# First transfers in another order, and the squares of x added in pairs on GpSimd

## The chip, the cores and the metric

The kernel runs on one core of a Trainium2 chip. What counts is its time on the device in microseconds (us), the median of several runs. The kernel before took 2918.81 us (three runs, 2916.25 to 2926.74).

## The reference

Two transformer layers follow each other over 1024 tokens of width 1024, in float32. The first, `hybrid_layer`, begins with a modulation that is worked out from a vector c, and with an RMS norm of x; everything else in it depends on the normed and modulated h:

```
mod = (jax.nn.silu(c) @ w_ada + b_ada)[:, None, :]
shift, scale, gate = jnp.split(mod, 3, axis=-1)
h = rms_norm(x, norm_g) * (1.0 + scale) + shift
(a_q, a_kv, ...) = jnp.split(h @ w_in, IN_OFFSETS, axis=-1)
```

`rms_norm` divides each token by the root of the mean of its squares over the 1024 channels. After that come four branches (compressed, selected and windowed attention; windowed attention with a sink; stick-breaking attention; retention), gated merges and an output product. The second layer has a convolution, forgetting attention, pooling, an output product, an MLP of width 4096 and a gated embedding. The change touches only what lies ahead of the first product with `w_in`.

## The kernel before, in words

Data lie transposed: channels on the 128 partitions, tokens along the row, so that x is eight chunks of 128 channels by 1024 tokens (`mm`). A dense product takes a block of weights (128 output channels) through all eight chunks. To reach float32 accuracy, weights and operand are each split in a rounded part and a rest (`whi`, `wlo`; `xhi`, `xlo`), and every product is three matmuls (`three`, L653). ScalarE makes `whi` from the landed block `raw` (L1112), GpSimd subtracts it from `raw` to make `wlo` (L1472).

Each engine has its own program; a list of events, `TIMELINE`, written out by `list_timeline`, gives all of them the same order after the start. The first event is `norm1`, then come the blocks `Dv0` and `Dv1`, interleaved by chunks. Semaphores connect the engines. Loads are issued by SyncE (SP) on one queue, in the order of its code; where SP waits for a semaphore, all later loads wait with it.

The start, ahead of `TIMELINE`, is what the change rewrites:

- SP loads the small vectors `vec`, the whole table `tab` (identity, ones, masks, distances, 2470 columns), the modulation weights `ada1` for the scale in two halves, x as one transfer, `ada0` for the shift in two halves, and the first weight block. The second weight block goes to the same place `raw` and waits until GpSimd has subtracted the first (`w_lo`); behind it stand `rtab` and the weights `ada2` of the gate.
- VectorE makes three bfloat16 masks (L1988 to L1990), then the products of the modulation: for each of eight chunks, `ada_sum` gains `ada` times an entry of silu(c) (L2004 first, then L2006). Between the fourth and the fifth product of `ada0` it waits for the root and takes its reciprocal (L1999).
- ScalarE squares the eight chunks of x into a ring of three buffers (`chunk_square`, L1132), then takes the root (`std`, L1139) and splits the first weight block.
- TensorE sums `ada_sum` over partitions (`modulation`, L986: eight matmuls with a column of ones), then the squares of each chunk as they come (`chunk_sum`, `square_sums`, L731: eight matmuls a chunk, each shown as two records), spreads the reciprocal root over the partitions (`broadcast`, L757) and sums the other modulation.
- In `norm1`, VectorE scales each chunk by the factor and the spread row (L2080), ScalarE adds the shift (L1402, L1397), and both with GpSimd make `xhi` and `xlo` (L2086, L1115, L1479).

Of the kernel before, what the change touches and what calls it, by code (L numbers as in the profile page):

```python
# [6 lines left out]
ALU = mybir.AluOpType  # L7
# [311 lines left out]

def table_layout():  # L320
    at, out = 0, {}
    for name, n in [("dist", S), ("ident", P), ("strict", P), ("tri", P), ("negones", P), ("ones", P),
                    ("up", P), ("low", P), ("cdist", NB * NCMP), ("cmask", NB * NCMP), ("gc", 2),
                    ("eps6", 1), ("eps5", 1), ("invw", 2), ("invc", 32)]:
        out[name] = (at, n)
        at += n
    return out, at


TABLES, NTABLE = table_layout()  # L330
VECS = {}
_at = 0
for _n, _w in [("c", 8), ("b_ada", 24), ("norm_g", 8), ("final_g", 8), ("g_mix_pre", 8), ("g_mix_post", 8),
# [10 lines left out]
def build(nc, xT, pT, wstream, wada, vecs, tables, rtables, cw1, cw2, wpw, wpool, out):  # L344
    with ExitStack() as ctx:
# [3 lines left out]
        def at(name, kib, shape, dt=F32):  # L349
            return nc.alloc_sbuf_tensor_at(name, shape, dt, offset=base + int(kib * 1024))  # L350
# [4 lines left out]
        def sem(name):  # L355
            return ctx.enter_context(nc.semaphore(name))
# [6 lines left out]
        ada1 = at("ada1", 32, [P, 8, D])  # L363
        mm = at("mm", 64, [P, NC, S])
        raw = at("raw", 96, [P, 10 * P])
        whi = [at("whi%d" % i, 101 + 5 * i, [P, 10, P], F32R) for i in range(2)]
        wlo = [at("wlo%d" % i, 111 + 5 * i, [P, 10, P], F32R) for i in range(2)]
        yhi = at("yhi", 121, [P, 2, S], F32R)
# [101 lines left out]
        res_dram = nc.dram_tensor("res_dram", [P, NC, S], F32, kind="Internal").ap()  # L470


        small_in, x_in, raw_in, rtab_in = (sem(n) for n in ("small_in", "x_in", "raw_in", "rtab_in"))
        ada_in = [[sem("ada_in%d%d" % (i, half)) for half in range(2)] for i in range(3)]
# [95 lines left out]
        @block.sync  # L570
        def _(sp):
            sp.dma_start(vec[:], vecs).then_inc(small_in, 16)
            sp.dma_start(tab[:], tables).then_inc(small_in, 16)
            for half in range(2):
                sp.dma_start(ada1[:, 4 * half:4 * half + 4, :], wada[1][:, 4 * half:4 * half + 4, :]
                             ).then_inc(ada_in[1][half], 16)
            sp.dma_start(mm[:], xT).then_inc(x_in, 16)
            for half in range(2):
                sp.dma_start(ada0[:, 4 * half:4 * half + 4, :], wada[0][:, 4 * half:4 * half + 4, :]
                             ).then_inc(ada_in[0][half], 16)  # L580

            def load_weights(b):
                if b >= 1:
                    sp.wait_ge(w_lo, b)
                n = BLOCK_LEN[b]
                src = wstream[BLOCK_OFF[b]:BLOCK_OFF[b] + P * n].rearrange("(p n) -> p n", p=P)
                sp.dma_start(raw[:, 0:n], src).then_inc(raw_in, 16)

            load_weights(0)
            load_weights(1)  # L590
            sp.dma_start(rtab[:], rtables).then_inc(rtab_in, 16)
            for half in range(2):
                sp.dma_start(ada2[half][:], wada[2][:, :, half * HALF:(half + 1) * HALF]).then_inc(ada_in[2][half], 16)
            for ev in TIMELINE:
                if ev[0] == "dense" and ev[2] == 2 and 1 < ev[1] + 1 < nblocks:
                    load_weights(ev[1] + 1)
                elif ev == ("cmp", 0):

                    sp.wait_ge(k_y, H)
                    sp.dma_start(cw1s[:], cw1).then_inc(cmp_in, 16)  # L600
                    sp.dma_start(cw2s[:], cw2).then_inc(cmp_in, 16)
                elif ev == ("dense", INDEX["o0"], 3):
                    for n in range(NC):
                        wait_split(sp, 1, n)
                        sp.dma_start(mm[:, n, :], xT[:, n, :]).then_inc(xres_in[n], 16)
                elif ev == ("dense", INDEX["Ecb1"], 4):
                    for n in range(NC):
                        sp.wait_ge(chunk_ready, n + 1)
                        sp.dma_start(res_dram[:, n, :], mm[:, n, :]).then_inc(res_out, 16)
                elif ev == ("conf", 0):  # L610

                    sp.wait_ge(s_norm, 128)
                    sp.dma_start(wpws[:], wpw).then_inc(pw_in, 16)
                    sp.dma_start(wpls[:], wpool).then_inc(pw_in, 16)
                elif ev[0] == "dense" and ev[2] == 3 and BLOCKS[ev[1]][1] == "x1":
                    sp.wait_ge(res_out, 16 * NC)
# [18 lines left out]
        def _(pe):  # L635
# [346 lines left out]
            def modulation(t):  # L982
# [122 lines left out]
        @block.scalar  # L1105
        def _(act):
            def split_weights(b):
                act.wait_ge(raw_in, 16 * (b + 1))
# [3 lines left out]
                nc.scalar.activation(flat(whi[b % 2])[:, 0:n], raw[:, 0:n], ACT.Copy).then_inc(w_hi, 1)  # L1112
# [12 lines left out]

            def chunk_square(j, n, src):

                if n < 3 and j:
                    act.wait_ge(nsum, (0, 4, 6)[j])
                if n >= 3:  # L1130
                    act.wait_ge(pq_used, 7 * j + n - 2)
# [334 lines left out]
        def _(pool):  # L1466
            tt = nc.gpsimd.tensor_tensor

            def split_weights(b):
                n = BLOCK_LEN[b]  # L1470
                pool.wait_ge(w_hi, b + 1)
                tt(flat(wlo[b % 2])[:, 0:n], raw[:, 0:n], flat(whi[b % 2])[:, 0:n].bitcast(F32),  # L1472
                   ALU.subtract).then_inc(w_lo, 1)

            def split_wide(v, pos, k, src):
# [27 lines left out]
            def window_sums():  # L1503
# [5 lines left out]
                for step in range(2):  # L1509
# [122 lines left out]
        def _(dve):  # L1632
# [359 lines left out]
            v.tensor_scalar(nsink[:], v_("sink"), -1.0, None, ALU.mult).then_inc(masks_done, 1)  # L1992

            def ada_products(t, tiles):

# [16 lines left out]

            dve.wait_ge(csil_done, 1)
            for t, a in ((1, ada1), (0, ada0)):
                ada_products(t, [[(slice(0, D), a[:, kc, :], kc // 4)] for kc in range(8)])
# [6 lines left out]
            for ev in TIMELINE:  # L2022
# [51 lines left out]
                elif ev[0] == "norm1":  # L2074
# [3 lines left out]
                    for n in range(NC + 1):  # L2078
# [4 lines left out]
                        if n and m % 2 == 0:  # L2083
# [3 lines left out]
                                                   in1=xhi[:, m, :].bitcast(F32), op0=ALU.add, op1=ALU.subtract  # L2087
                                                   ).then_inc(x_lo2, 1)
                    applied(0, x_src, 8)
                elif ev[0] == "split_merged":  # L2090
                    for n in range(NC):
                        split_wide(1, n, n, mm[:, n, :])
# [235 lines left out]
```

## Time and profile before

| | |
|---|---|
| median of 3 runs | 2918.81 us |
| the profiled execution | 2915.78 us, its span 2913.8 us |
| TensorE busy | 2709.8 us (93%) |
| VectorE, ScalarE, GpSimd busy | 922.2, 817.1, 872.8 us |
| granted TensorE clock, mean | 0.949 of full speed |
| first 72 us: TensorE, VectorE busy | 38.61, 28.06 us |
| first 72 us: GpSimd busy | 5.19 us |

The profile is of one execution; its own time is that of the span and what lies around it. Starts are counted from the start of the span. PEclk is the granted clock of TensorE in parts of full speed. In the rows, `x8` is a count of records, "idle before" is how long the engine had nothing to do, and the name behind the arrow is what ended that.

### The profile page before, as it was taken

The page shows a single profiled execution, that of the slowest core. Times are in us where ns is not written, and L with a number is a line of the kernel's source. Part 1 is how long each engine was busy: PE and PEld are TensorE (multiplying, and loading weights), DVE is VectorE, ACT ScalarE, POOL GpSimd, SP SyncE. Part 2 cuts the span into 40 slices and gives each one's busy share as a digit, 9 for nine tenths or more (in the row PEclk, how much of TensorE's full clock was granted, in tenths as well). Part 3 has the DMA queues.
Part 4 walks back from the last instruction along what each step waited for, and adds up shares of the span by engine and source line. Part 5 has one row for each costly group of instructions (what it writes and reads, how often), then busy time and mean ns, then how long its engine had stood idle before and what let it go on. Part 6 is the DMA issues. An engine that isn't in the chain of part 4 may idle for free.

```text
span 2913.8 us, 30462 instructions
## 1 busy us (share of the span) xinstructions
PE 2709.8 (93%) x12660; PEld 2179.4 (75%) x12660; DVE 922.2 (32%) x1431; ACT 817.1 (28%) x1218; POOL 872.8 (30%) x492
## 2 busy tenths in 40 slices
PE   5899899999998999999999899878999999999896
PEld 5677778766677777778778677667888888888785
DVE  3312441233301354520225656423112222222423
ACT  2201452344321343431232333323211111111321
POOL 0211211344321111124552211235333333333633
PEclk9988999999998897999989999989999999999998
DMA  6101101100011000001212000120111111111111
GB/s 252 62 18 37 37 26 44 35 28 19 15 38 56 12 16 19 16 28 46 97 41 101 29 15 22 35 87 29 44 51 44 51 44 53 49 51 44 56 37 67
DMA packets 33432, 134.84 MB, mean 46 GB/s; under 512 B 3536, under 2 KB 3856, under 8 KB 32400
## 3 DMA queue, kind: packets, MB, share of 16 engines
q1 hardware_dynamic: 32976, 131.85, 13.1%
q8 instruction: 101, 1.65, 0.2%
q10 hardware_dynamic: 320, 1.05, 0.1%
q14 instruction: 35, 0.29, 0.0%
HBM read 123.45 MB, written 8.39 MB: 45 GB/s over the span
## 4 chain that ended last, share of the span: by engine, by line
PE 87%; DVE 6%; ACT 3%; POOL 2%; issue 2%; DMA 1%; SPq 0%; POOLq 0%; ACTq 0%; DVEq 0%
PE slot L653 54%; PE slot L699 12%; PE ps L864 4%; PE ps L835 3%; PE ps L731 3%; PE ps L813 2%; PE ps L897 1%; PE ps L888 1%; PE ps L901 1%; PE ps L914 1%; DVE cacc L2068 1%; DMA mm<-xT 1%; DVE ada_sum L2006 1%; PE ps L757 1%; POOL wlo L1472 1%
## 5 line engine op out<-in xcount | busy, mean ns | idle before, releaser
L653 PE MATMUL slot<-xhi,whi 128*128 128x512 f32 x2192 | 715.6, 408 | 57.3 <-ACT zs L1203 16.9
L653 PE MATMUL slot<-xlo,whi 128*128 128x512 f32 x2192 | 693.0, 398 | 0.0
L653 PE MATMUL slot<-xhi,wlo 128*128 128x512 f32 x2192 | 690.1, 397 | 0.0
L1472 POOL TENSOR_TENSOR wlo<-raw,whi 128x1024 fp32r<-128x1024 f32 (+1 forms) x169 | 429.2, 2539 | 860.3 <-ACT whi L1112 860.3
L653 PEld LDWEIGHTS slot<-xhi,whi 128*128 128x128 f32 x2192 | 406.9, 194 | 146.4 <-issue 64.7
L653 PEld LDWEIGHTS slot<-xhi,wlo 128*128 128x128 f32 x2192 | 421.3, 192 | 92.2
L653 PEld LDWEIGHTS slot<-xlo,whi 128*128 128x128 f32 x2192 | 421.4, 192 | 91.6
L1112 ACT ACTIVATE whi<-raw 128x1024 fp32r<-128x1024 f32 (+1 forms) x169 | 186.1, 1101 | 321.6 <-PE slot L699 174.4
L699 PE MATMUL slot<-uhi,whi 128*128 128x512 f32 x512 | 158.4, 391 | 0.0
L699 PE MATMUL slot<-ulo,whi 128*128 128x512 f32 x512 | 157.9, 390 | 0.0
L699 PE MATMUL slot<-uhi,wlo 128*128 128x512 f32 x512 | 157.7, 389 | 0.0
L835 PEld LDWEIGHTS ps<-brv,pbuf 128*128 128x128 f32 x936 | 129.8, 200 | 20.0 <-ACT cb L1344 5.8
L1544 POOL TENSOR_TENSOR ulo<-tbuf,uhi 128x1024 fp32r<-128x1024 f32 x32 | 77.7, 2430 | 220.9 <-ACT uhi L1252 220.9
L1771 DVE TENSOR_TENSOR mm<-slot,mm 128x1024 f32<-128x1024 f32 x56 | 68.6, 1224 | 229.3 <-PE slot L699 228.3
L1759 DVE SCALAR_TENSOR_TENSOR tbuf<-slot,tab 128x1024 f32<-128x1024 f32 x32 | 39.2, 1224 | 302.4 <-PE slot L653 302.3
L835 PE MATMUL ps<-brv,pbuf 128*128 128x64 f32 x936 | 124.8, 277 | 5.6 <-ACT cb L1344 3.3
L1281 ACT ACTIVATE pbuf<-ps 128x512 f32<-128x512 f32 (+3 forms) x176 | 79.5, 452 | 178.2 <-PE ps L813 176.8
L1530 POOL TENSOR_TENSOR mm<-mm,zs 128x1024 f32<-128x1024 f32 x24 | 58.1, 2419 | 227.7 <-DVE zs L1683 227.7
L1252 ACT ACTIVATE uhi<-tbuf 128x1024 fp32r<-128x1024 f32 x32 | 33.9, 1060 | 297.0 <-DVE tbuf L1762 297.0
L699 PEld LDWEIGHTS slot<-uhi,whi 128*128 128x128 f32 x512 | 95.5, 188 | 22.3 <-issue 3.0
L699 PEld LDWEIGHTS slot<-uhi,wlo 128*128 128x128 f32 x512 | 96.1, 188 | 20.1
L699 PEld LDWEIGHTS slot<-ulo,whi 128*128 128x128 f32 x512 | 96.1, 188 | 20.0
(308 smaller groups left out, 3155.6 us busy)
## 6 DMA issues: line engine op xcount, KB each, us to landing
raw<-wstream SPq DMA_DIRECT2D x129, 512.0 KB, 3.2
raw<-wstream SPq DMA_DIRECT2D x40, 640.0 KB, 3.9
ada<-wada SPq DMA_DIRECT2D x6, 2048.0 KB, 16.1
mm<-xT SPq DMA_DIRECT2D x1, 4096.0 KB, 24.1
mm<-xT SPq DMA_DIRECT2D x8, 512.0 KB, 4.9
res_dram<-mm SPq DMA_DIRECT2D x8, 512.0 KB, 4.1
res<-res_dram SPq DMA_DIRECT2D x8, 512.0 KB, 6.5
outT<-res SPq DMA_DIRECT2D x8, 512.0 KB, 2.6
```

The source lines that it names most:

```text
L653: o = mm_(outs[:, half * HALF:(half + 1) * HALF], w[b % 2][:, k_w, :], x[:, k_x, half * HALF:(half + 1) * HALF], start=first and j == 0, s ...
L699: o = mm_(slot[(g + t) % 2][:, half * HALF:(half + 1) * HALF], w[:, kc, t, :], x[:, kc, half * HALF:(half + 1) * HALF], start=kc == 0 and ...
L731: o = mm_(ps7[:, place * NB + tb:place * NB + tb + 1], src[:, tb * P:(tb + 1) * P], t_("ones", 0, 1), start=first and tb == 0, stop=last a ...
L813: o = nc.tensor.transpose(ps6[:, (c - 4 * bi) * P:(c - 4 * bi + 1) * P], sring[m % 3][:, c * P:(c + 1) * P], t_("ident"))
L835: o = mm_(ps7[:, 0:DH], ptr[:, c * P:(c + 1) * P], v, start=c == 0, stop=c == nb - 1)
L864: o = mm_(ps4[:, c0:c1], q_[r0:r0 + DH, :], k_[r0:r0 + DH, lo * P + c0:lo * P + c1], start=j == 0, stop=j == 2)
L1112: nc.scalar.activation(flat(whi[b % 2])[:, 0:n], raw[:, 0:n], ACT.Copy).then_inc(w_hi, 1)
L1281: nc.scalar.activation(ptr[:, bi * HALF:bi * HALF + w], ps6[:, 0:w], ACT.Copy).then_inc(s_ptsb, 1)
L1472: tt(flat(wlo[b % 2])[:, 0:n], raw[:, 0:n], flat(whi[b % 2])[:, 0:n].bitcast(F32), ALU.subtract).then_inc(w_lo, 1)
L1530: tt(mm[:, n, :], mm[:, n, :], zs[0][:], ALU.add).then_inc(sum_done, 1)
L1544: tt(ulo[:, n, :], tbuf[n % 2][:], uhi[:, n, :].bitcast(F32), ALU.subtract).then_inc(u_lo, 1)
L1771: v.tensor_tensor(mm[:, n, :], slot[gg % 2][:], mm[:, n, :], ALU.add).then_inc(slot_free[gg % 2], 1)
```

## The change

The table's columns are laid out anew, so that what the start needs (identity, ones, constants) comes first, 294 columns (`EARLY`). SP now loads `vec`, these columns, x in two halves, `ada1` in four parts of two chunks, `ada0` in five parts (the last two of one chunk each), the first weight block, the second into a place of its own (`raw1`) and without a wait, the rest of the table, `rtab`, `ada2`. Each part has its semaphore.

ScalarE squares the chunks into four buffers. GpSimd adds two squared chunks in place, four times. TensorE sums the four pairs, ahead of the first modulation (`first_sums`). VectorE's masks are made behind the first norm, when the rest of the table is there.

```
-            for half in range(2):
-                sp.dma_start(ada1[:, 4 * half:4 * half + 4, :], wada[1][:, 4 * half:4 * half + 4, :]
-                             ).then_inc(ada_in[1][half], 16)
-            sp.dma_start(mm[:], xT).then_inc(x_in, 16)
...
+            sp.dma_start(tab[:, 0:EARLY], tables[:, 0:EARLY]).then_inc(small_in, 16)
             for half in range(2):
+                sp.dma_start(mm[:, 4 * half:4 * half + 4, :], xT[:, 4 * half:4 * half + 4, :]).then_inc(x_in[half], 16)
+            for t, a in ((1, ada1), (0, ada0)):
+                for part, (k0, k1) in enumerate(ADA_PARTS[t]):
+                    sp.dma_start(a[:, k0:k1, :], wada[t][:, k0:k1, :]).then_inc(ada_in[t][part], 16)

             def load_weights(b):
-                if b >= 1:
+                if b >= 2:
                     sp.wait_ge(w_lo, b)
...
-                sp.dma_start(raw[:, 0:n], src).then_inc(raw_in, 16)
+                sp.dma_start((raw1 if b == 1 else raw)[:, 0:n], src).then_inc(raw1_in if b == 1 else raw_in, 16)
             load_weights(0)
             load_weights(1)
+            sp.dma_start(tab[:, EARLY:NTABLE], tables[:, EARLY:NTABLE]).then_inc(tab_in, 16)
...
+            def first_sums():
+                for pair in range(4):
+                    pe.wait_ge(x_paired, pair + 1)
+                    square_sums(0, (sbuf[0], pbuf[0])[pair % 2], pair == 0, pair == 3
+                                ).then_inc(x_summed if pair < 3 else nsum, 1)
...
+            first_sums()
             modulation(1)
-            for n in range(NC):
-                chunk_sum(0, 0, n)
             broadcast(0)
...
-            act.wait_ge(x_in, 16)
             for n in range(NC):
-                chunk_square(0, n, mm[:, n, :])
+                if n % 4 == 0:
+                    act.wait_ge(x_in[n // 4], 16)
+                if n >= 4 and n % 2 == 0:
+                    act.wait_ge(x_summed, n // 2 - 1)
+                nc.scalar.activation((sbuf + pbuf)[n % 4][:], mm[:, n, :], ACT.Square).then_inc(pq_done, 1)
...
+            for pair in range(4):
+                a, b = (sbuf, pbuf)[pair % 2]
+                pool.wait_ge(pq_done, 2 * pair + 2)
+                tt(a[:], a[:], b[:], ALU.add).then_inc(x_paired, 1)
             split_weights(0)
...
             dve.wait_ge(small_in, 32)
-            link(v.tensor_copy(identb[:], t_("ident")))
-            link(v.tensor_copy(upb[:], t_("up")))
-            link(v.tensor_copy(lowb[:], t_("low")))
...
                     applied(0, x_src, 8)
+                    dve.wait_ge(tab_in, 16)
+                    link(v.tensor_copy(identb[:], t_("ident")))
+                    link(v.tensor_copy(upb[:], t_("up")))
+                    link(v.tensor_copy(lowb[:], t_("low")))
```

The queue of SP at the start of the program before; `ada1` and `ada0` are the modulation weights, `mm` is x, `raw` a weight block, and a shape is partitions by columns:

```order
L572 DMA vec_118<-vecs 128x207
L573 DMA tab_117<-tables 128x2470
L575 DMA ada1_53<-wada 128x4096 x2
L577 DMA mm_54<-xT 128x8192
L579 DMA ada0_52<-wada 128x4096 x2
L587 DMA raw_55<-wstream 128x1024 x2
L591 DMA rtab_64<-rtables 128x1024
L593 DMA ada20_99<-wada 128x8x512
L593 DMA ada21_100<-wada 128x8x512
```

Of these rows, the second of the two `raw` loads waits for `w_lo`. The same queue at the same place in the changed kernel:

```order
L578 DMA vec_119<-vecs 128x207
L579 DMA tab_118<-tables 128x294
L581 DMA mm_54<-xT 128x4096 x2
L584 DMA ada1_53<-wada 128x2048 x4
L584 DMA ada0_52<-wada 128x2048 x3
L584 DMA ada0_52<-wada 128x1024 x2
L591 DMA raw_55<-wstream 128x1024
L591 DMA raw1_56<-wstream 128x1024
L595 DMA tab_118<-tables 128x2176
L596 DMA rtab_65<-rtables 128x1024
L598 DMA ada20_100<-wada 128x8x512
L598 DMA ada21_101<-wada 128x8x512
```

x moved ahead of `ada1`, the larger part of the table behind the second weight block, and no load here waits any more.

GpSimd's first operations in the program before; `wlo` is the rest of a weight block, `xlo` that of x:

```order
L1472 TENSOR_TENSOR wlo0_58<-raw_55,whi0_56 128x1024
L1472 TENSOR_TENSOR wlo1_59<-raw_55,whi1_57 128x1024
L1479 TENSOR_TENSOR xlo_50<-mm_54,xhi_49 128x1024 x4
L1472 TENSOR_TENSOR wlo0_58<-raw_55,whi0_56 128x1024
L1472 TENSOR_TENSOR wlo1_59<-raw_55,whi1_57 128x1024
```

The last two rows are the third and the fourth weight block. The same engine at the same place in the changed kernel:

```order
L1541 TENSOR_TENSOR sbuf0_73<-sbuf0_73,sbuf1_74 128x1024
L1541 TENSOR_TENSOR pbuf0_75<-pbuf0_75,pbuf1_76 128x1024
L1541 TENSOR_TENSOR sbuf0_73<-sbuf0_73,sbuf1_74 128x1024
L1541 TENSOR_TENSOR pbuf0_75<-pbuf0_75,pbuf1_76 128x1024
L1490 TENSOR_TENSOR wlo0_59<-raw_55,whi0_57 128x1024
L1490 TENSOR_TENSOR wlo1_60<-raw1_56,whi1_58 128x1024
L1497 TENSOR_TENSOR xlo_50<-mm_54,xhi_49 128x1024 x4
```

Four additions of squares stand ahead of the first two subtractions, of which the second reads `raw1`.

## Rows read from the trace of the kernel before

**Rows 1.** The chain of waits in order: start us, us, what.

```profile
2.66 24.07 DMA mm<-xT
...
26.76 1.06 ACT sbuf L1132
...
27.87 27.48 PE ps L731 x128
...
55.37 0.28 ACT rms L1139
...
57.12 3.26 DVE ada_sum L2006
...
63.07 2.99 PE ps L986 x16
...
67.17 1.29 DVE mm L2080
...
71.16 23.38 PE slot L653 x96
```

**Rows 2.** ScalarE's timeline, squares: start, us, engine, line, operation, count, idle before.

```profile
26.76 2.00 ACT L1132 ACTIVATE sbuf<-mm 128x1024 f32<-128x1024 f32 x2 [19.29 <-DMA mm<-xT]
...
34.89 1.06 ACT L1132 ACTIVATE sbuf<-mm 128x1024 f32<-128x1024 f32 x1 [2.36 <-PE ps L731]
```

**Rows 3.** VectorE's timeline, modulation products and the reciprocal.

```profile
12.23 0.75 DVE L2004 TENSOR_SCALAR ada_sum<-ada,csil 128x1024 f32<-128x1024 f32 x1 [3.88 <-DMA ada<-wada]
...
31.65 0.75 DVE L2004 TENSOR_SCALAR ada_sum<-ada,csil 128x1024 f32<-128x1024 f32 x1 [9.28 <-DMA ada<-wada]
...
55.74 0.20 DVE L1999 RECIPROCAL rrms<-rms 128x8 f32<-128x8 f32 x1 [19.37 <-ACT rms L1139]
```

**Rows 4.** DMA issues of the first 72 us: count, KB each, us to landing.

```profile
ada<-wada SPq DMA_DIRECT2D x6, 2048.0 KB, 16.1
mm<-xT SPq DMA_DIRECT2D x1, 4096.0 KB, 24.1
...
tab<-tables SPq DMA_DIRECT2D x1, 1235.0 KB, 6.0
```

**Rows 5.** Lines L2006 (up to 72 us) and L2080: duration ns minimum/median/maximum.

```profile
L2006 DVE SCALAR_TENSOR_TENSOR ada_sum<-ada,csil,ada_sum x14: 1233/1285/3248, 13.0 to 61.7; 128x1024 f32<-128x1024 f32 x14
...
L2080 DVE SCALAR_TENSOR_TENSOR mm<-mm,gmul,ps x8: 1268/1272/1279, 67.2 to 80.4; 128x1024 f32<-128x1024 f32 x8
```

**Rows 6.** GpSimd's timeline, the first two subtractions.

```profile
56.66 2.63 POOL L1472 TENSOR_TENSOR wlo<-raw,whi 128x1024 fp32r<-128x1024 f32 x1 [56.15 <-ACT whi L1112]
64.09 2.34 POOL L1472 TENSOR_TENSOR wlo<-raw,whi 128x1024 fp32r<-128x1024 f32 x1 [4.79 <-ACT whi L1112]
```

**Rows 7.** Line L2068, the convolution's taps: duration ns minimum/median/maximum.

```profile
L2068 DVE SCALAR_TENSOR_TENSOR cacc<-cu,vec,cacc x60: 1230/1261/3394, 1570.1 to 1830.0; 128x994 f32<-128x994 f32 x2, 128x995 f32<-128x995 f32 x2, 128x996 f32<-128x996 f32 x2, 128x997 f32<-128x997 f32 x2
```

**Rows 8.** SP's timeline: the two weight blocks, the wait of the second included.

```profile
4.65 54.99 SPq L587 DMA_DIRECT2D raw<-wstream  x2
```

**Rows 9.** Timeline behind the first dense stage: ScalarE's third weight block, VectorE's next work.

```profile
89.18 1.06 ACT L1112 ACTIVATE whi<-raw 128x1024 fp32r<-128x1024 f32 x1 [5.28 <-PE slot L653]
...
95.44 1.22 DVE L1798 COPY dv<-slot 128x1024 f32<-128x1024 f32 x1 [11.68 <-PE slot L717]
```

**Rows 10.** VectorE's timeline, the first mask.

```profile
7.26 0.23 DVE L1988 CAST identb<-tab 128x128 bf16<-128x128 f32 x1 [7.26 <-DMA tab<-tables]
```

**Rows 11.** TensorE's timeline: broadcast, the gate's modulation sums, the dense product behind them.

```profile
55.99 3.79 PE L757 MATMUL ps<-tab,rrms 128*128 128x128 f32 x16 [0.66 <-DVE rrms L1999]
...
148.02 3.55 PE L986 MATMUL ps<-tab,ada_sum 128*128 128x1 f32 x16 [15.52 <-DVE ada_sum L2006]
...
155.84 0.66 PE L653 MATMUL slot<-xhi,wlo 128*128 128x512 f32 x2
```

**Rows 12.** Windows of the first dense stage; behind the bracketed columns PEclk, DMA share, GB/s.

```profile
71.16:73.90 2.74, 2.74 (x7) 2.16 (x8) 2.71 (x3) 2.37 (x3) 1.91 (x1) 0.50 1.05 400
73.90:94.00 20.10, 20.10 (x90) 16.65 (x89) 9.80 (x8) 10.46 (x10) 10.09 (x5) 1.00 0.21 77
```

More of the change, by code:

```diff
@@ L321, in table_layout @@
     at, out = 0, {}
-    for name, n in [("dist", S), ("ident", P), ("strict", P), ("tri", P), ("negones", P), ("ones", P),
-                    ("up", P), ("low", P), ("cdist", NB * NCMP), ("cmask", NB * NCMP), ("gc", 2),
-                    ("eps6", 1), ("eps5", 1), ("invw", 2), ("invc", 32)]:
+    for name, n in [("ident", P), ("ones", P), ("gc", 2), ("eps6", 1), ("eps5", 1), ("invw", 2), ("invc", 32),
+                    ("strict", P), ("tri", P), ("negones", P), ("up", P), ("low", P), ("cdist", NB * NCMP),
+                    ("cmask", NB * NCMP), ("dist", S)]:
         out[name] = (at, n)
@@ L330 @@
 TABLES, NTABLE = table_layout()
+EARLY = TABLES["strict"][0]
+ADA_PARTS = [[(0, 2), (2, 4), (4, 6), (6, 7), (7, 8)], [(0, 2), (2, 4), (4, 6), (6, 8)]]
 VECS = {}
@@ L365, in build @@
         raw = at("raw", 96, [P, 10 * P])
+        raw1 = at("raw1", 177, [P, 8 * P])
         whi = [at("whi%d" % i, 101 + 5 * i, [P, 10, P], F32R) for i in range(2)]
@@ L470, in build @@
         res_dram = nc.dram_tensor("res_dram", [P, NC, S], F32, kind="Internal").ap()
-        small_in, x_in, raw_in, rtab_in = (sem(n) for n in ("small_in", "x_in", "raw_in", "rtab_in"))
-        ada_in = [[sem("ada_in%d%d" % (i, half)) for half in range(2)] for i in range(3)]
+        small_in, tab_in, raw_in, raw1_in, rtab_in = (
+            sem(n) for n in ("small_in", "tab_in", "raw_in", "raw1_in", "rtab_in"))
+        x_paired, x_summed = sem("x_paired"), sem("x_summed")
+        x_in = [sem("x_in%d" % half) for half in range(2)]
+        ada_in = [[sem("ada_in%d%d" % (i, part)) for part in range((5, 4, 2)[i])] for i in range(3)]
         xres_in = [sem("xres_in%d" % n) for n in range(NC)]
@@ L572, in _ @@
             sp.dma_start(vec[:], vecs).then_inc(small_in, 16)
-            sp.dma_start(tab[:], tables).then_inc(small_in, 16)
+            sp.dma_start(tab[:, 0:EARLY], tables[:, 0:EARLY]).then_inc(small_in, 16)
             for half in range(2):
-                sp.dma_start(ada1[:, 4 * half:4 * half + 4, :], wada[1][:, 4 * half:4 * half + 4, :]
-                             ).then_inc(ada_in[1][half], 16)
-            sp.dma_start(mm[:], xT).then_inc(x_in, 16)
-            for half in range(2):
-                sp.dma_start(ada0[:, 4 * half:4 * half + 4, :], wada[0][:, 4 * half:4 * half + 4, :]
-                             ).then_inc(ada_in[0][half], 16)
+                sp.dma_start(mm[:, 4 * half:4 * half + 4, :], xT[:, 4 * half:4 * half + 4, :]).then_inc(x_in[half], 16)
+            for t, a in ((1, ada1), (0, ada0)):
+                for part, (k0, k1) in enumerate(ADA_PARTS[t]):
+                    sp.dma_start(a[:, k0:k1, :], wada[t][:, k0:k1, :]).then_inc(ada_in[t][part], 16)
             def load_weights(b):
-                if b >= 1:
+                if b >= 2:
                     sp.wait_ge(w_lo, b)
@@ L1107, in split_weights @@
             def split_weights(b):
-                act.wait_ge(raw_in, 16 * (b + 1))
+                if b == 1:
+                    act.wait_ge(raw1_in, 16)
+                else:
+                    act.wait_ge(raw_in, 16 * max(1, b))
                 if b >= 2:
@@ L1111, in split_weights @@
                 n = BLOCK_LEN[b]
-                nc.scalar.activation(flat(whi[b % 2])[:, 0:n], raw[:, 0:n], ACT.Copy).then_inc(w_hi, 1)
+                nc.scalar.activation(flat(whi[b % 2])[:, 0:n], (raw1 if b == 1 else raw)[:, 0:n], ACT.Copy
+                                     ).then_inc(w_hi, 1)
             def split_wide(k, src):
@@ L1126, in chunk_square @@
             def chunk_square(j, n, src):
-                if n < 3 and j:
+                if n < 3:
                     act.wait_ge(nsum, (0, 4, 6)[j])
-                if n >= 3:
-                    act.wait_ge(pq_used, 7 * j + n - 2)
+                else:
+                    act.wait_ge(pq_used, 7 * (j - 1) + n - 2)
                 nc.scalar.activation(sring[n % 3][:], src, ACT.Square).then_inc(pq_done, 1)
@@ L1471, in split_weights @@
                 pool.wait_ge(w_hi, b + 1)
-                tt(flat(wlo[b % 2])[:, 0:n], raw[:, 0:n], flat(whi[b % 2])[:, 0:n].bitcast(F32),
+                tt(flat(wlo[b % 2])[:, 0:n], (raw1 if b == 1 else raw)[:, 0:n], flat(whi[b % 2])[:, 0:n].bitcast(F32),
                    ALU.subtract).then_inc(w_lo, 1)
@@ L1987, in _ @@
             dve.wait_ge(small_in, 32)
-            link(v.tensor_copy(identb[:], t_("ident")))
-            link(v.tensor_copy(upb[:], t_("up")))
-            link(v.tensor_copy(lowb[:], t_("low")))
             link(v.memset(token[:], 1.0))
-            v.tensor_scalar(nsink[:], v_("sink"), -1.0, None, ALU.mult).then_inc(masks_done, 1)
             def ada_products(t, tiles):
@@ L2014, in _ @@
             for t, a in ((1, ada1), (0, ada0)):
-                ada_products(t, [[(slice(0, D), a[:, kc, :], kc // 4)] for kc in range(8)])
+                ada_products(t, [[(slice(0, D), a[:, kc, :], sum(k1 <= kc for _, k1 in ADA_PARTS[t]))]
+                                 for kc in range(8)])
             dve.wait_ge(mod_mm, 1)
@@ L2089, in _ @@
                     applied(0, x_src, 8)
+                    dve.wait_ge(tab_in, 16)
+                    link(v.tensor_copy(identb[:], t_("ident")))
+                    link(v.tensor_copy(upb[:], t_("up")))
+                    link(v.tensor_copy(lowb[:], t_("low")))
+                    v.tensor_scalar(nsink[:], v_("sink"), -1.0, None, ALU.mult).then_inc(masks_done, 1)
                 elif ev[0] == "split_merged":
```

## Prediction

> **What bounds the kernel now.** I began with the busy shares: TensorE is busy for 93% of the span, so time is to be won only where it waits. The chain of waits says where that is: it starts with 71 us in which no dense product runs, and from there goes from one dense product to the next [rows 1]. The change touches only those 71 us, so I read them row by row.
>
> The chain goes through x: it lands at 26.73, ScalarE's first square takes 1.06, then TensorE's column sums fill 27.87 to 55.34, then the root, its reciprocal, the last four products of `ada0`, a column sum, four short vector operations, the first norm row and the first dense product at 71.16 [rows 1]. Each of the eight chunks costs TensorE about 3.43 (27.48 / 8). ScalarE waits 2.36 before most squares for one of three buffers [rows 2]; TensorE is the limit there.
>
> VectorE's view shows when things land, by when its waits end: first half of `ada1` at 12.23, first half of `ada0` at 31.65 [rows 3]. The transfers land in the order of issue: from 12.23 to 26.73 there are 2048 + 4096 KB [rows 4], so 4.83 per 2048 KB; the next 2048 KB take 4.92. I use 4.85. VectorE then stands idle, with `ada0` in place, for 19.37 until the root is there [rows 3].
>
> One row of the chain matters more than its size: the product at 57.12 took 3.26 [rows 1] where the median of the fourteen products is 1.29 [rows 5]. GpSimd's subtraction of the weights ran from 56.66 to 59.29 [rows 6]. The product ends 1.09 after it: VectorE stood still, and the collision cost 3.26 - 1.29 = 2.0. The taps of the later convolution, of the same shape and with both inputs in SBUF, show the same spread, 1.26 median and 3.39 at most [rows 7].
>
> **The change part by part.**
>
> *Transfers.* Ahead of x now stand `vec` and 294 columns of the table (147 KB) where `vec`, 1235 KB and 2048 KB were ahead of the first landing at 12.23. By the end of x's first half 1088 KB less have moved than by that landing: 1088 / 2048 * 4.85 = 2.6 less, so it lands at 9.6, the second half at 14.5, then `ada1` in four parts at 16.9, 19.3, 21.8, 24.2, `ada0` at 26.6, 29.1, 31.5, 32.7, 33.9, the two weight blocks at 35.1 and 36.3, the rest of the table at 39, `rtab` at 40, `ada2` by 50. Before, the SP queue stood at the second weight block until 59.6 for GpSimd [rows 8], with `rtab` and `ada2` behind it; that wait is gone. Nobody needs these early: they are first used after the first dense stage. The third weight block still waits for two subtractions and now stands behind `ada2`, landing at about 51; ScalarE asks for it only when block 0 has been used up (at 89.18 before [rows 9], some 72 after). The three masks on VectorE (0.23 each [rows 10]) go behind the first norm; there VectorE sat idle for 11.68 before its next work [rows 9], which hides them. Cost nothing.
>
> *Squares and sums.* Eight squares stay, 0.95 apart [rows 2]. New are four additions on GpSimd of 128x1024; the trace has no such addition here, the nearest row is the subtraction of the same size, 2.34 alone [rows 6], and I take 2.35. Sums on TensorE fall from eight to four: 4 * 3.43 = 13.7. Squares 0 and 1 are done at 11.7, pair 0 at 14.1, its sum at 17.5; squares 4 and 5 wait for that sum and end at 19.6; pair 1 is summed by 21.0; squares 6 and 7 end at 23.0. Pairs 2 and 3 need the port that VectorE uses, end at about 22.8 and 26.1, and the last sum ends at 29.8. The root is there at 30.1 instead of 55.6. So 25.5 go from this part, and it is no longer what ends last.
>
> *What is late next: VectorE.* Its sixteen products cannot start before 16.9, and the additions and subtractions on GpSimd collide with them. From the third product, at 19.3, they run without a gap, since each part lands before it is asked for: 13 products of 1.285 plus 0.025 between [rows 5], 17.0; one of 0.75 [rows 3], 0.8; the reciprocal, 0.25; together 18.1. Four collisions lie inside: pairs 2 and 3, and the subtractions of blocks 0 (raw there at 35.1, copy 1.05) and 1. Block 0's was the one collision of before; block 1's ran behind the products, at 64.09 [rows 6], and now comes among them since its weights no longer wait. At 2.0 each that is 8.0. VectorE ends at 19.3 + 18.1 + 8.0 = 45.4. Bounds of one collision: nothing, as the first norm row beside GpSimd (whose row input is in PSUM) took 1.27 throughout [rows 5], and 2.13, the longest of the taps [rows 7]. I take 2.0, the row of this very operation.
>
> TensorE does `modulation(1)` (3.55 [rows 11]) from 31.1, the broadcast (3.79) from about 36, both before 40, and waits for VectorE: 2.99 to 3.55 for `modulation(0)` [rows 1, 11], then 1.1 from its end to the first norm row [rows 1]. That row starts at 45.4 + 3.2 + 1.1 = 49.7 instead of 67.17.
>
> *The dense stage.* From the norm row to the first product 3.99 stay [rows 1]. Before, TensorE's granted clock was 0.50 (1.2 GHz) for the first 2.7 of it and then 1.00 (2.4 GHz), after an idle time of 5.1, from the end of the modulation sums [rows 1, 12]. Now it idles about 5 before the last modulation sums and about 5 after; I expect the same start. A matmul took 2.74 / 7 = 0.39 at the lower level and 20.10 / 90 = 0.22 at the higher [rows 12], so 2.7 more or less at the lower level move 7 matmuls by 0.17: 1.2 either way.
>
> **Sum.** 67.17 - 49.7 = 17.5 less. The profiled execution was 2915.78 (span 2913.8 and 2.0 around it), giving 2898.3. It lies 3.0 below the median of the three runs (2918.81) and close to the fastest (2916.25); for the median of new runs the sum gives 2901.3 by the old median. I forecast 2900.
>
> **Rivals.**
>
> *The port costs less.* Without collisions VectorE follows the transfers: its work ends at 45.4 - 8.0 = 37.4 by the same count. TensorE's own order is level with it: pair 3 at 25.4, its sum 28.9, modulation 32.4, broadcast 36.2. The norm row comes at 37.4 + 3.2 + 1.1 = 41.7: 25.5 less, 2890. For it: sixteen products on before's path met only one GpSimd operation. Against: that one cost the full 2.0, and GpSimd has work exactly when VectorE has no gap.
>
> *Less than half a per cent comes of it.* TensorE's early work is thinned, from 27.5 of unbroken sums to 13.7. If the lower clock lasts 10 into the dense stage, 7.3 longer, that is 19 matmuls at 0.17, 3.2, and the gain is 14.3: 2903. For it: after the later idle time of 15.5 the lower level lasted until 155.8, some 8 into the work [rows 11]. Against: in these 8 lie 3.5 of narrow sums; the wide products alone again took 4.3.
>
> *Slower: x does not land first.* Sixteen transfers are out before the first half of x lands, instead of seven. If the engines spread over all that is queued, x's last bytes come with the last of 20 MB, at 50. The pipeline of squares, pairs and sums runs from there: first sum at 54, last at about 69, root and broadcast to 73, modulation 76, norm row 77: 10 later than before, 2926. It decides from the point where x's second half lands after about 40. Against: with seven out, everything landed in order of issue [rows 3, 8]. The Trainium skill (DMA: Bandwidth & Descriptors, Queues, rings and completion order) says that completion is not first-in, first-out per issuing engine. In this trace it was, to within 0.1 of 4.85 per 2048 KB.
>
> **How the numbers follow.** Forecast (VectorE and the port set the end, 15 to 20 less, its own range 2896 to 2904) 0.70; port costs less (20 to 26 less) 0.15; under half a per cent 0.12; slower 0.03. Half a per cent, 14.6 us, is about what runs of this kernel can tell from no change. The forecast lies 3 above that bound and the runs shown spread by 10, so a part of it can be measured as "same": faster 0.62 + 0.14 = 0.76, same 0.08 + 0.01 + 0.12 = 0.21, slower 0.03. The range from 2889 (the port free, by the profiled time) to 2909 (10 less than the median) leaves out the slow case and the tails.
>
> **What would show it.** Right: x's two waits on ScalarE end near 9.6 and 14.5; four groups of sums on TensorE end near 30; products on VectorE of over 3 us beside each GpSimd operation from 20 on; the first modulation sums run behind the square sums; first dense product at 53 to 54; from there every row as before, 17 to 18 earlier. Wrong: products at 1.3 beside GpSimd, or a root later than 36, which would make TensorE's sums the bound still; a third weight block that ScalarE waits for; a lower clock beyond 57.

## The result and the profile after

The changed kernel took 2897.24 us (median of four runs, 2895.66 to 2898.39), the kernel before 2918.87 beside it (four runs, 2916.25 to 2926.74). The ratio is 0.9921 (95% interval 0.9901 to 0.9941): 21.6 less, where 2900 was forecast. The profiled execution took 2895.66 with a span of 2893.9, against 2915.78 and 2913.8: the two profiled executions lie 20.1 apart, their spans 19.9.

The chain of waits of the changed kernel, to be read beside [rows 1] (start, us, what):

```profile
3.14 16.03 DMA ada<-wada
...
19.26 1.29 DVE ada_sum L2024
...
20.58 3.27 DVE ada_sum L2024
...
23.88 3.26 DVE ada_sum L2024
...
37.13 3.27 DVE ada_sum L2024
...
40.43 3.26 DVE ada_sum L2024
...
45.05 3.59 PE ps L998 x16
...
49.54 1.29 DVE mm L2099
...
53.53 24.05 PE slot L658 x96
```

x, the sums and the root have left the chain. It now goes from one part of `ada1` through VectorE's products, without a gap, to the modulation sums, and four of the products take 3.26 or 3.27 instead of 1.29. The first dense product starts at 53.53 instead of 71.16. The same products in VectorE's timeline, where the six before the second modulation and the last four stand in one row each:

```profile
19.26 11.83 DVE L2024 SCALAR_TENSOR_TENSOR ada_sum<-ada,csil,ada_sum 128x1024 f32<-128x1024 f32 x6 [0.37 <-DMA ada<-wada]
...
35.87 9.12 DVE L2024 SCALAR_TENSOR_TENSOR ada_sum<-ada,csil,ada_sum 128x1024 f32<-128x1024 f32 x4
```

TensorE's timeline, the sums of the pairs; start, us, engine, line, operation, count, idle before:

```profile
13.90 3.55 PE L736 MATMUL ps<-tab,sbuf 128*128 128x1 f32 x16 [13.90 <-POOL sbuf L1541]
17.31 3.55 PE L736 MATMUL ps<-tab,pbuf 128*128 128x1 f32 x16
22.81 3.57 PE L736 MATMUL ps<-tab,sbuf 128*128 128x1 f32 x16 [1.95 <-POOL sbuf L1541]
26.24 3.55 PE L736 MATMUL ps<-tab,pbuf 128*128 128x1 f32 x16
31.14 3.58 PE L998 MATMUL ps<-tab,ada_sum 128*128 128x1 f32 x16 [1.35 <-DVE ada_sum L2024]
```

There are four groups in place of eight, in front of the modulation; each still takes some 3.5, and they end at 29.8.

GpSimd's timeline:

```profile
11.41 2.35 POOL L1541 TENSOR_TENSOR sbuf<-sbuf,sbuf 128x1024 f32<-128x1024 f32 x1 [10.90 <-ACT sbuf L1334]
13.72 2.34 POOL L1541 TENSOR_TENSOR pbuf<-pbuf,pbuf 128x1024 f32<-128x1024 f32 x1
19.63 3.13 POOL L1541 TENSOR_TENSOR sbuf<-sbuf,sbuf 128x1024 f32<-128x1024 f32 x1 [3.57 <-ACT sbuf L1334]
22.98 3.07 POOL L1541 TENSOR_TENSOR pbuf<-pbuf,pbuf 128x1024 f32<-128x1024 f32 x1 [0.22 <-ACT pbuf L1334]
36.59 5.99 POOL L1490 TENSOR_TENSOR wlo<-raw,whi 128x1024 fp32r<-128x1024 f32 x2 [10.55 <-ACT whi L1126]
```

The first two additions, with VectorE still waiting, take 2.35. The other two and the two subtractions stand beside the four long products of the chain and take 2.7 to 3.3 each: when both want the port, both lose. The Trainium skill (SBUF — State Buffer, Who interferes with whom) says that a VectorE instruction with two SBUF inputs contends with a GpSimd instruction that reads SBUF, over a shared port pair that is an exclusive lock. The 3.26 beside the 1.29 agrees.

SP's timeline, to be read beside [rows 8]:

```profile
2.66 3.51 SPq L584 DMA_DIRECT2D ada<-wada  x7
6.22 2.61 SPq L584 DMA_DIRECT2D ada<-wada  x1
8.87 3.31 SPq L584 DMA_DIRECT2D ada<-wada  x1
12.21 4.24 SPq L591 DMA_DIRECT2D raw<-wstream  x2
...
19.13 18.54 SPq L598 DMA_DIRECT2D ada<-wada  x2
```

There is no wait in SP's code over this stretch. Seven issues of `ada` took 3.51 together, 0.5 each and little more than those ahead of them; the next two took 2.61 and 3.31, and the last two 18.54 together. SP was held back, from its twelfth transfer on.

The dense stage's first matmuls on TensorE:

```profile
53.53 1.19 PE L658 MATMUL slot<-xhi,whi 128*128 128x512 f32 x2 [4.92 <-DVE xlo L2105]
...
56.23 1.05 PE L658 MATMUL slot<-xhi,whi 128*128 128x512 f32 x2
57.09 0.94 PE L658 MATMUL slot<-xlo,whi 128*128 128x512 f32 x2
57.87 0.63 PE L658 MATMUL slot<-xhi,wlo 128*128 128x512 f32 x2
```

The first pair of matmuls is followed after 1.00, the next three after 0.85, the fifth after 0.78, and all later ones after 0.46: the lower level of the clock lasted 4.3 here, against 2.7 before [rows 12]. The whole piece of 96 took 24.05 instead of 23.38. So the stage ends 94.54 - 77.58 = 17.0 earlier.

### The profile page after: what moved, and what is told of

Same layout as the page of the kernel before. It is cut to its first block, busy times and chain, and to the rows that moved or that the text cites. A ratio compares the mean times of both kernels' runs of the same rounds, so it can differ in the third digit from the quotient of the medians.

```text
span 2893.9 us, 30346 instructions
## 1 busy us (share of the span) xinstructions
PE 2694.4 (93%) x12596; PEld 2162.7 (75%) x12596; DVE 929.3 (32%) x1431; ACT 816.7 (28%) x1218; POOL 884.8 (31%) x496
## 4 chain that ended last, share of the span: by engine, by line
PE 86%; DVE 7%; ACT 3%; POOL 2%; issue 2%; DMA 1%; SPq 0%; POOLq 0%; ACTq 0%; DVEq 0%
PE slot L658 54%; PE slot L704 12%; PE ps L876 4%; PE ps L847 3%; PE ps L825 2%; PE ps L736 2%; PE ps L909 1%; PE ps L900 1%; DVE ada_sum L2024 1%; PE ps L913 1%; PE ps L926 1%; DVE cacc L2087 1%; POOL wlo L1490 1%; DMA ada<-wada 1%; PE ps L769 1%
## 5 line engine op out<-in xcount | busy, mean ns | idle before, releaser
L704 PEld LDWEIGHTS slot<-uhi,wlo 128*128 128x128 f32 x512 | 96.1, 188 | 20.1
L704 PEld LDWEIGHTS slot<-ulo,whi 128*128 128x128 f32 x512 | 96.1, 188 | 20.1
```

Of the source, the lines that this page charges most:

```text
L704: o = mm_(slot[(g + t) % 2][:, half * HALF:(half + 1) * HALF], w[:, kc, t, :], x[:, kc, half * HALF:(half + 1) * HALF], start=kc == 0 and ...
```

## The experiments

**Theories.** *Port*: x, pairs and sums are off the path; VectorE's products and four collisions with GpSimd at 2.0 each set the start of the dense stage; later stages follow unchanged. *Landing*: the products are long because of the transfers that land beside them, and GpSimd has no part in it. *Sums*: TensorE's square sums are still the bound, so that the pairs bring what they save there (four groups of 3.43). *Start of the clock*: what is left of the difference hangs on how long TensorE runs at its lower level at the start of the dense stage. The measure is the start of the first dense product (71.16 before, 53.53 after), beside the time. The first four experiments stood beside a kernel before of 2917.21 (thirteen runs, 2913.17 to 2921.96), the later four beside 2916.48 (seven runs, 2914.66 to 2924.99).

### The new transfers without the pairs

```
-            first_sums()
+            for n in range(NC):
+                chunk_sum(0, 0, n)
             modulation(1)
...
-            for pair in range(4):
-                a, b = (sbuf, pbuf)[pair % 2]
-                pool.wait_ge(pq_done, 2 * pair + 2)
-                tt(a[:], a[:], b[:], ALU.add).then_inc(x_paired, 1)
```

> The new transfers and the new order on TensorE, but the squares as before: eight chunks in a ring of three buffers, summed one by one, nothing added on GpSimd. Measure: the start of the first dense product (71.16 before, 53.53 in the changed kernel). Theory 'port' (VectorE's products, from the third one on without a gap, set the end, and each GpSimd operation beside them costs 2.0): first sum starts at 10.4, eight sums of 3.43 end at 37.9, root at 38.3; the first twelve products now meet nothing and are done at 32, wait for the root, the last four then meet the two subtractions of weights: 38.5 + 5.2 + 4.0 = 47.7 at most, 45.7 if only one falls among them; first dense product at 54 to 56, within 2.5 of the changed kernel: the pairs alone bring little. Theory 'sums' (the halving of the sums is where the gain is): the root comes 8.5 later than in the changed kernel (29.8), and so does the first dense product, at 62.

2901.39 (2896.67 to 2902.43, four runs), ratio 0.9944 (0.9929 to 0.9959). The dense stage starts at 55.50. VectorE's timeline:

```profile
19.46 7.89 DVE L2019 SCALAR_TENSOR_TENSOR ada_sum<-ada,csil,ada_sum 128x1024 f32<-128x1024 f32 x6 [0.37 <-DMA ada<-wada]
...
38.56 0.20 DVE L2012 RECIPROCAL rrms<-rms 128x8 f32<-128x8 f32 x1 [6.55 <-ACT rms L1155]
38.68 9.12 DVE L2019 SCALAR_TENSOR_TENSOR ada_sum<-ada,csil,ada_sum 128x1024 f32<-128x1024 f32 x4
```

Six products take 7.89 where no GpSimd addition runs (11.83 in the changed kernel). VectorE then waits 6.55 for a root that comes at 38.5, 8.4 later than with the pairs, and the last four products meet the two subtractions. The first dense product moves by only 1.97. That is *port*; by *sums* it would have been 62. Of the 17.6, the new transfers with their order bring 15.7 by themselves. The pairs bring the root 8.4 forward and take away VectorE's wait of 6.55, but they put two more collisions on it, 3.94 (11.83 - 7.89). The products end 2.81 later without the pairs (47.80 against 44.99); 0.83 of that is made up again, as the modulation sums behind them took 2.74 here and 3.57 in the changed kernel.

### The pairs alone, with the old transfers

```
             modulation(1)
-            for n in range(NC):
-                chunk_sum(0, 0, n)
+            first_sums()
...
+            for pair in range(4):
+                a, b = (sbuf, pbuf)[pair % 2]
+                pool.wait_ge(pq_done, 2 * pair + 2)
+                tt(a[:], a[:], b[:], ALU.add).then_inc(x_paired, 1)
```

> The pairs alone: transfers, their order and the masks as in the kernel before, squares added by pairs on GpSimd, four sums on TensorE. Both theories: x lands at 26.7, last sum at 46, root at 46.3, the last four products from 46.5 with one subtraction among them end at 53.8, first dense product at 62, that is 9 less than before. Theory 'port' adds: pairs 0 and 1 run at 28.8 to 33.5, beside the first four products of ada0, which then show one or two of over 3 us but stay hidden behind the root. Were the sums not the bound before, the product would stay at 71.

2910.71 (2903.96 to 2917.81, ten runs), ratio 0.9977 (0.9967 to 0.9988). The dense stage starts at 63.32, 7.8 earlier than before. TensorE's timeline:

```profile
31.07 3.58 PE L732 MATMUL ps<-tab,sbuf 128*128 128x1 f32 x16 [5.18 <-POOL sbuf L1532]
...
43.54 3.55 PE L732 MATMUL ps<-tab,pbuf 128*128 128x1 f32 x16
47.76 3.79 PE L765 MATMUL ps<-tab,rrms 128*128 128x128 f32 x16 [0.66 <-DVE rrms L2012]
54.83 3.57 PE L994 MATMUL ps<-tab,ada_sum 128*128 128x1 f32 x16 [3.29 <-DVE ada_sum L2019]
```

With x late, the sums set the end and halving them shows: here the pairs are worth 7.8, where 9 were expected. The last sum ends at 47.1 instead of 46, and the modulation sums took 3.57. On VectorE one operation was held up by the pairs: the scaling of 0.75 took 2.39, and not over 3, beside the second addition (31.0 to 33.3), hidden ahead of the root as *port* has it. Each part alone brings 15.7 and 7.8, both together 17.6 and not 23.5. For the root the two do add up: it comes 17.2 and 8.2 earlier by one part alone and 25.5 by both. But VectorE's products reach it only at 35.75 in the changed kernel, when it has been there since 30.1.

### GpSimd's two subtractions behind VectorE's products

```
+            pool.wait_ge(ada_acc, 2)
             split_weights(0)
```

> The changed kernel with one wait more: GpSimd starts the two subtractions of weights only when all sixteen products are done. Theory 'port': two of the four products of over 3 us become 1.3, VectorE's last product ends at 41.0 instead of 45.0, the subtractions run from 41 to 46, still ahead of the first dense product, which starts at 49.5 instead of 53.5. Theory 'landing' (transfers pace the products, and the long ones are long because of what lands): nothing moves, or the later subtractions make it later.

2894.68 (2892.10 to 2897.59, four runs), ratio 0.9924 (0.9906 to 0.9941). VectorE's timeline:

```profile
36.05 5.20 DVE L2025 SCALAR_TENSOR_TENSOR ada_sum<-ada,csil,ada_sum 128x1024 f32<-128x1024 f32 x4
...
43.72 0.17 DVE L2038 TENSOR_TENSOR mod<-ps,vec 128x16 f32<-128x16 f32 x1
43.93 2.06 DVE L2039 TENSOR_SCALAR gmul<-mod 128x8 f32<-128x8 f32 x1
```

GpSimd's two subtractions:

```profile
41.33 4.64 POOL L1490 TENSOR_TENSOR wlo<-raw,whi 128x1024 fp32r<-128x1024 f32 x2 [15.10 <-DVE ada_sum L2025]
```

TensorE, the modulation sums and the first dense matmuls:

```profile
41.30 1.95 PE L998 MATMUL ps<-tab,ada_sum 128*128 128x1 f32 x16 [1.33 <-DVE ada_sum L2025]
50.28 1.19 PE L658 MATMUL slot<-xhi,whi 128*128 128x512 f32 x2 [7.03 <-DVE xlo L2106]
```

The four products take 5.20 instead of 9.12: two collisions of 1.96 are gone, as *port* has it; by *landing* nothing would have moved. But the dense stage starts at 50.28 and not at 49.5: the small operation on 128x8 took 2.06 (0.17 elsewhere) beside the second subtraction, which ran from 43.6 to 46.0. That it is not 51.4 comes from the modulation sums, 1.95 here and 3.57 in the changed kernel. The operation just before the held one, with one of its inputs in PSUM, took its 0.17 beside the same subtraction. The collision cost 1.89 on 128x8 and 1.96 on 128x1024: it does not shrink with VectorE's operation.

### The changed kernel again

> The changed kernel once more, to see how far the stages behind the start drift from run to run. If the 2.5 us beyond the 17.6 of the start come from TensorE's granted clock in later stages and not from the change, then against the first profile of the same kernel single stages are again up to 3 us earlier or later, while the first dense product starts at 53.5 within 0.3.

2897.41 (2896.32 to 2898.45, four runs), ratio 0.9933 (0.9918 to 0.9948). Its trace has a span of 2896.2, and a first dense product at 53.79; from there TensorE's timeline:

```profile
53.79 1.19 PE L658 MATMUL slot<-xhi,whi 128*128 128x512 f32 x2 [4.92 <-DVE xlo L2105]
...
59.05 1.00 PE L658 MATMUL slot<-xhi,whi 128*128 128x512 f32 x2
59.89 0.62 PE L658 MATMUL slot<-xlo,whi 128*128 128x512 f32 x2
```

Seven slow pairs this time, not five: ScalarE takes up the first result at 78.72, where it was 77.61 in the other execution of the same kernel, 1.1 later with a start 0.26 later. From there to the end, ScalarE's instructions, taken one by one, start between 1.7 us earlier (at 764) and 3.7 later (at 2718) than in the other trace, and the spans differ by 2.3. That is how far two executions of one kernel wander against each other behind the first stage. Where they part, the granted clock differs: it is 0.91 against 0.68 from 280 to 290, about where the repeat gains 2.6, and 0.75 against 1.00 from 1130 to 1140, about where it loses 2.9.

### Two additions more on GpSimd

```
+            for _ in range(2):
+                link(tt(sbuf[1][:], sbuf[1][:], sbuf[1][:], ALU.add))
             split_weights(0)
```

> The changed kernel with two additions more on GpSimd behind the fourth pair, on a buffer that nobody needs. Theory 'port': they fall among VectorE's products (from 26 to 31), two more products take over 3, the last product ends 4.0 later (49.0 instead of 45.0) and the first dense product starts at 57.5 instead of 53.5. Theory 'landing' (the products are paced by what lands): all parts land when they did, so nothing moves.

One execution, 2901.95; the first dense product starts at 56.34. GpSimd's two additions, then VectorE's six products that four of the additions lie beside:

```profile
25.87 5.70 POOL L1543 TENSOR_TENSOR sbuf<-sbuf 128x1024 f32<-128x1024 f32 x2
```

```profile
19.13 14.84 DVE L2026 SCALAR_TENSOR_TENSOR ada_sum<-ada,csil,ada_sum 128x1024 f32<-128x1024 f32 x6 [0.37 <-DMA ada<-wada]
```

The six take 14.84 instead of 11.83, and the dense stage comes 2.8 later. Work on GpSimd that nothing waits for lengthens the path, as *port* says; under *sums* or *landing* it would not have. The price was 1.5 apiece ((14.84 - 11.83) / 2), not the 2.0 expected. These additions were done 1.75 after VectorE's product ahead of them had ended, those of the pairs 2.2 after it. They read one buffer twice, where the others read two; whether that is the reason was not tried.

### The second weight block waits again

```
-                if b >= 2:
+                if b >= 1:
                     sp.wait_ge(w_lo, b)
```

> The changed kernel, with the second weight block waiting again until the first is subtracted (39), and the rest of the table, rtab and ada2 queued behind it, as before. Theory 'port': the block lands at 42.4, its subtraction starts at 43.5 when the products are done, so only three of them collide: last product at 43.0, first dense product at 51.5, that is 2.0 earlier although a load comes later. Theory 'landing': later loads make nothing earlier; 53.5 or more.

One execution, 2901.20, the first dense product at 51.92. VectorE's last four products and GpSimd's second subtraction:

```profile
36.23 7.16 DVE L2024 SCALAR_TENSOR_TENSOR ada_sum<-ada,csil,ada_sum 128x1024 f32<-128x1024 f32 x4
```

```profile
44.27 2.34 POOL L1490 TENSOR_TENSOR wlo<-raw,whi 128x1024 fp32r<-128x1024 f32 x1 [4.61 <-ACT whi L1126]
```

A block that comes later starts the dense stage 1.6 earlier: three collisions instead of four. *Landing* is out. The four products are 1.96 shorter, and 0.36 of it is lost because they began later in this trace. The time of this single execution lies above all eight of the changed kernel (2895.66 to 2898.45). In its trace ScalarE's instructions start 1.2 to 1.5 earlier than in the changed kernel's from 70 to 1240, and fall behind after that, by up to 6.9: what was lost was not lost at the start. Whether the 1.6 shows in the time, one execution can't tell.

### The subtractions behind the products, and apart

```
             pool.wait_ge(ada_acc, 2)
             split_weights(0)
+            pool.wait_ge(mod_done, 1)
```

> As the version with the later subtractions, but the second one only when the factor for the norm rows is made. There a small operation on the factor (128x8) took 2.06 behind the second subtraction where it takes 0.17 alone. Theory 'port': it takes 0.17 again, the first norm row starts at 44.4 and the first dense product at 48.4, 1.9 earlier than with both subtractions behind the products (50.28) and 5.1 earlier than in the changed kernel; the median is 5 less, which is at the edge of what rounds can tell. If the small operation is long for another reason (its input in PSUM, a wait for TensorE), it stays at 50.3.

2893.16 (2891.33 to 2894.45, four runs), ratio 0.9914 (0.9897 to 0.9931). TensorE's timeline:

```profile
40.96 3.57 PE L998 MATMUL ps<-tab,ada_sum 128*128 128x1 f32 x16 [1.33 <-DVE ada_sum L2026]
49.44 1.19 PE L658 MATMUL slot<-xhi,whi 128*128 128x512 f32 x2 [4.91 <-DVE xlo L2107]
```

No long operation is left on VectorE behind the two beside pairs 2 and 3, and the small one takes 0.17 again. Against the third experiment 1.9 should have been gained (50.28 to 48.4), and 0.84 came: the modulation sums took 3.57, where they had taken 1.95 there. The same sums, after the same wait of 1.33, ran at either of two speeds.

### Five useless matmuls ahead of the dense stage

On top of the kernel just shown, five products of the identity with the distance table, into a place that the dense stage writes anew:

```
             modulation(0).then_inc(mod_mm, 1)
+            pe.wait_ge(tab_in, 16)
+            for _ in range(5):
+                mm_(slot[1][:, 0:HALF], t_("ident"), t_("dist", 0, HALF), start=True, stop=True)
```

> The version before, with five matmuls of no use (128x512, identity by a table, into an accumulator that is not in use yet) on TensorE between the last modulation sums and the first dense product, where it was idle for 5 to 7. If the slow first 3 us of the dense stage come from the lower clock after the idle time, the first dense matmuls take 0.62 a pair from the start, instead of 1.05 for the first three to four pairs, and the stage ends 1.3 to 1.7 earlier by the same start. If they are slow because their operands are still being made (VectorE and GpSimd write xlo beside them), nothing moves.

2889.17 (2888.16 to 2899.81, four runs), ratio 0.9900 (0.9880 to 0.9920). TensorE's timeline:

```profile
44.33 6.48 PE L1008 MATMUL slot<-tab 128*128 128x512 f32 x10
50.24 1.03 PE L658 MATMUL slot<-xhi,whi 128*128 128x512 f32 x2
51.11 0.62 PE L658 MATMUL slot<-xlo,whi 128*128 128x512 f32 x2
```

With the wait filled, one pair is slow instead of three, while the operands are made beside them as before: the slow start is the clock's. That standing still is enough for it, the third experiment shows: its sums had run at the faster speed (1.95), TensorE then stood still for 7.03, and the first four pairs were slow, with a granted clock of 0.51. The five overran the wait, though, and the dense stage starts 0.8 later (50.24 against 49.44); ScalarE takes up the first result at 72.65 against 72.85, so that the stage is 1.0 shorter, where 1.3 to 1.7 were expected. The profiled execution is the slowest of the four, 2899.81; the other three took 2888.16 to 2890.00. Of the 4.0 between the two medians the first stage shows only that 0.2, and the intervals of the two ratios overlap: that this version is faster than the one without the five matmuls is not shown. Both have lower medians than the changed kernel: 2893.16 and 2889.17 beside 2897.24 and 2897.41; the intervals of the ratios overlap with its own.

## Why the prediction was right, and where its steps were off

*Transfers.* Right. The squares begin at 9.33 (predicted 9.6 for x's first half), the first product at 16.82 (16.9), the third at 19.26 (19.3). The masks are hidden as costed. One of them even took 2.30 beside a subtraction of GpSimd in the norm, and VectorE still had 9.41 idle behind it, against 11.68 [rows 9]. ScalarE took up the third weight block at 72.22, after a wait for TensorE and not for the load.

*Squares and sums.* Right. The last pair is done at 26.05 (26.1), the sums at 29.79 (29.8), the root at 30.1. The part "25.5 go from this part" was a statement on the root and not on the time, and the first experiment shows how far apart these are: with the new transfers but without pairs the root comes at 38.5, and the dense stage only 1.97 later than with them.

*Four collisions.* Right in number, place and price: 3.27, 3.26, 3.27, 3.26, an excess of 1.97 each. The products end at 45.0 (45.4). The taps that the price was compared with are 128x994 to 128x997 [rows 7], nearly and not quite of the same shape. Moving two of them (third experiment), adding two (fifth) and removing one (sixth) each moved the dense stage in the direction that this step gives, by 3.25 of 4.0, 2.8 of 4.0 and 1.6 of 2.0.

*The modulation behind them.* Mis-sized: 3.57, where 3.2 was taken, at the upper end of the two rows. The first norm row starts at 49.54 (49.7), as the two errors nearly cancel, which is luck.

*The start of the dense stage.* The clock was expected as before, with 1.2 either way. The lower level lasted five pairs and not three, and cost 0.67 (24.05 - 23.38). When the same kernel ran again it lasted seven, and the stage was 0.85 longer still (1.11 - 0.26), 1.5 over the kernel before: more than the 1.2 allowed. A lower clock beyond 57 was named as a sign of being wrong; it lasted to 57.87 and to 59.89. So this step was off in size; the sum came out because it weighs little. What sets the number of slow pairs is open: TensorE stood still for 5.12, 4.92, 4.92 and 4.91 ahead of three, five, seven and three of them (before, changed, repeated, seventh experiment). The rival that put this at 3.2, and the whole gain under half a per cent, had the direction and not the size.

*From there on.* "Every row as before, 17 to 18 earlier" is only right on average. The first stage ends 17.0 earlier, but at later points the same rows lie 15.7 to 21.2 earlier, and 19.9 at the end of the span. The repeated run, with 17.6 at its end, shows that two executions of one kernel differ by as much. So the 17.5 of the sum and the 19.9 of the trace are the same within what one pair of traces can tell. The median of 21.6 less has the same spread in it, and how much of the 4.0 beyond the 17.6 is the change's own can't be told from these runs. It is these 4.0 that put the time below the 2901.3 of the sum; no step of the prediction accounts for them.

*The rivals.* By the number alone, 21.6 less falls among the 20 to 26 less of the rival with the cheaper port. The rows decide against it: the port cost its full price, and the first dense product came at 53.53, inside the 53 to 54 of the forecast. The slower rival rested on sixteen transfers being out before x lands, instead of seven before (eight with the first weight block, which the count leaves out). SP's rows show eleven issued by 6.2 and the twelfth by 8.8, when x's first half was there at 9.33. Its premise was wrong by four, and with twelve out everything still landed in the order of issue.

## What to carry to other kernels

When a change shortens the work that sets the end, ask for the next engine, and price what the change itself puts beside that engine: here the pairs on GpSimd took 13.7 of sums off TensorE, and moved the dense stage by 2.0. What two parts take off the same wait counts only until another engine ends last, so each is to be tried alone. A load or a piece of side work that comes earlier is not free when its follow-up work lands on a port of the bound engine: put it behind, and check the small operations there as well.

## What the runs showed of the hardware

- A VectorE operation on 128x8 with one tensor input took 2.06 in place of 0.17 beside a GpSimd subtraction on 128x1024 (third experiment). Small size was no protection there; one on 128x16 with an input in PSUM kept its 0.17.
- Beside the long products the collision is paid on both sides: GpSimd's 2.35 became 2.7 to 3.3 in the changed kernel. In the third experiment, where VectorE's operation was small, the two subtractions took 4.64 together, no longer than alone.
- SP's issues took 0.39 to 0.52 apiece for the first eleven transfers and 2.61 and 3.31 for the next two. The two halves of `ada2` held SP for 18.54, and what stood behind them in its code could not be issued before 37.7; here that cost nothing, as the third weight block waits for GpSimd until 42.6. Everything landed in the order of issue.
- Two rows of TensorE in the changed kernel, the sums of squares of a later norm:

```profile
1480.62 1.84 PE L736 MATMUL ps<-tab,pbuf 128*128 128x1 f32 x16
...
1488.94 3.55 PE L736 MATMUL ps<-tab,sqr 128*128 128x1 f32 x16
```

The same sixteen records take 1.84 directly behind dense products, with a granted clock of 1.00, and 3.55 after 8 us of nothing but such sums and a pause of 0.79, with one of 0.50. All sums of the first 50 us of this kernel take 3.55 to 3.58, and the first pairs of dense matmuls start about 0.85 apart, though the granted clock of this stretch is shown as 1.00. The same stretch, the modulation sums, in the changed kernel and in its repeat; behind the bracketed columns PEclk, DMA share, GB/s:

```profile
45.00:49.00 4.00, 3.57 (x16) 3.49 (x16) 0.31 (x2) 0.00 (x0) 0.00 (x0) 1.00 1.05 387
```

```profile
45.00:49.00 4.00, 3.57 (x16) 3.49 (x16) 0.33 (x2) 0.00 (x0) 0.00 (x0) 0.50 1.05 388
```

The same sums take the same 3.57, and the column says 1.00 in one trace and 0.50 in the other, where it had already changed once (0.80 from 41 to 44). By these durations TensorE ran at 1.2 GHz in both: ahead of its first change in a trace the column can't be read as the clock.
